# First norm of a two-block fp32 transformer kernel: loaded and turned by quarters, its scale applied behind the products

## The chip, the cores and the metric

The kernel runs on one core of a Trainium2 chip. The time is the device time of one execution in microseconds (us), and the median of several runs counts. In the rows PE is TensorE, PEld its weight load, DVE VectorE, ACT ScalarE, POOL GpSimd and SP SyncE; SPq and POOLq are the queues that issue DMAs. L12 is line 12 of the kernel.

## What is computed

Two transformer blocks on 256 tokens of width 2048, all in fp32. The change touches the start of the first block:

```
u = rmsnorm(h, norm_mix_g[l])            # x * rsqrt(mean(x*x) + eps) * g, per token
z = u @ w_in[l]
b_a, c_a, v_a, q, k, v, gl_a, gl_b = jnp.split(z, SPLIT_POINTS, axis=-1)
y_a = (b_a * centred_dwconv3(c_a * v_a, conv_a_w[l])) @ w_out_a[l]
q = rope(q, s); k = rope(k, s)
att = banded_window_attention(q, k, v, sink_logits[l])
g_a = sigmoid(gl_a + b_gate[:D]);  g_b = sigmoid(gl_b + b_gate[D:])
h = h + (g_a * y_a + g_b * (att @ w_o_attn)) @ w_mix_out
```

Behind it stand the norm, a feed-forward part with a convolution, and a second block with an expert layer. They are not touched.

## The kernel before, in words

**Products by units.** All weights pass through one stream of 1096 units. A unit is 128x1024 fp32 values (512 KB). SP loads it to RAW (5 buffers, L288); ScalarE rounds it to HI (L293); VectorE writes the rest, raw minus HI, to LO (L294). HI and LO have 4 buffers each. TensorE multiplies a unit by the activations, themselves held as a high and a low half (XH and XL in XX), in three passes: L368 to L370 where tokens lie on the partitions of the result (q, k, v), L378 to L380 where channels do. `product` runs over the units of one group of 512 columns, 8 units for 2048 rows, into one of two pairs of banks. A unit by token is 12 matmuls of 512 columns.

**What sets the order.** Each engine has one queue that runs strictly in order, and the program is written out once. Before the matmuls of unit i stand in the queue, `prepare(i + LOOK)` puts HI and LO of the units up to i+3 into the queues of ScalarE and VectorE (LOOK = 3). After each unit `step` adds one piece of the generators in `evacuations`, `beside` and `background`. A product is followed by what takes its banks away.

**The start.** SP loads x in two halves by tokens (L225), the identity (L226) and the norm's factors for all partitions (L227), then the first five units. POOL waits for the factors and loads constants, parameters and small tensors (L228, L229, L233). ScalarE sums the squares of both halves (`squares`, L467), `scale_of` and `rstd` make y, the reciprocal root, on two numbers per partition (L497, L452 to L458). `normed` then works by quarters of the width: VectorE forms x times y times the factors in UN (`scaled`, L503), TensorE turns four 128x128 blocks for each half of the tokens (L527), ScalarE copies the high half to XX (L533), VectorE the low half (L534). All four quarters come before the first unit.

**The first products.** Two products make q, one makes k and v. Behind each, `rope` rotates with four VectorE operations for each half of the tokens (L778, L779, L781, L783), by the tables cos and sin in CONST. For k and v a copy of k (L798) and ScalarE's copy of v (L799) follow. Then come, for each of two halves of the convolution, c (ScalarE copies it to CT, L822), v_a (multiplied with CT to PR, L825), three taps (L830, L813, L815), and b_a (L834); then four products with the gates of the first branch (`gate`: ScalarE's sigmoid from the banks, L842), the product with w_out_a, and for the second branch gate and attention output by turns. The attention runs between the units as `background`. `turned` and `spread` are there for the later norms: `turned` multiplies a quarter by the factors without y and turns it, `spread` makes y a row for all partitions by a diagonal (L568) and two matmuls (L574) into RS (L579).

Of the kernel before, what the change touches and what calls it, by code (L numbers as in the profile page):

```python
# [12 lines left out]
ALU = mybir.AluOpType  # L13
# [96 lines left out]
def _program(nc, a, out, ctx):  # L110
# [101 lines left out]
    def landing(name):  # L212
        return [sem(name), 0]

    l_x = landing("l_x")
    l_xt = [landing(f"l_x{t}") for t in range(2)]
    l_ident, l_const, l_par, l_small, l_gb, l_gb1, l_bi, l_gb2, l_keys, l_out = [landing("l_" + n) for n in (
# [10 lines left out]
    m_const = PO.dma(lambda e: e.dma_start(CONST[:, 128:N_CONST], a["consts"][:, 128:N_CONST]), l_const, m_gb)  # L228
    m_par = PO.dma(lambda e: e.dma_start(PAR[:], a["params"]), l_par, m_gb)  # L229
    for dst, src in ((SINK[:, 0, :], rows(a["sinks"][0])), (SINK[:, 1, :], rows(a["sinks"][1])),  # L230
                     (QKG[:, 0, :], rows(a["qkg"][0])), (QKG[:, 1, :], rows(a["qkg"][1])),
                     (POSI[:], a["pos"])):
        m_small = PO.dma(lambda e, dst=dst, src=src: e.dma_start(dst, src), l_small)  # L233


    units = []
# [41 lines left out]
    landed, hi_done, lo_done, mm_done = [], [], [], []  # L278

    def prepare(n):  # L280

        while len(hi_done) <= min(n, len(units) - 1):
            i = len(hi_done)
            while len(landed) <= min(i + NRAW - 1, len(units) - 1):
                j = len(landed)
                free = [hi_done[j - NRAW], lo_done[j - NRAW]] if j >= NRAW else None
                src, w = units[j]
                landed.append(SP.dma(lambda e, j=j, src=src, w=w: e.dma_start(RAW[:, j % NRAW, 0:w], src),  # L288
                                     l_raw[j % NRAW], free))
# [56 lines left out]
    def product(by_token, nk, xh, xl, ready, k0=0, width=512, turn=0):  # L346
# [44 lines left out]
    def product_both(ready, dst, rest, free):  # L391
# [149 lines left out]
    def turned(g, gb, m_in, m_g, free, marks, m_un, m_un_read):  # L541
# [7 lines left out]
        for t in range(2):  # L549
            i, b, fr = spare()  # L550

            def fn(e, t=t, b=b):
                for j in range(4):
                    m = e.transpose(b[:, 128 * j:128 * j + 128], UN[:, t, 512 * g + 128 * j:512 * g + 128 * j + 128],
                                    ident)
                return m

            m = PE.do(fn, m_u[t], fr)
# [209 lines left out]
    turn = un[:, 3072:3584]  # L768
    cosv, sinv = (const(n).rearrange("p (t c) -> p t c", t=2) for n in ("cos", "sin"))
    m_rope = []  # L770

    def rope(dst, src, t, nh, m):
# [13 lines left out]
    for g in range(2):  # L786
        pair, banks, m = product(True, 16, XH, XL, x_ready)
        free = []
        for t in range(2):
            r, _ = rope(q_tok[:, t, 512 * g:512 * g + 512].rearrange("p (h d) -> p h d", d=64),  # L790
                        banks[t].rearrange("p (h d) -> p h d", d=64), t, 8, m)
            free.append(r)
        acc_free[pair] = free
    pair, banks, m = product(True, 16, XH, XL, x_ready)
    free = []
    for t in range(2):
        r, w = rope(k_tok[:, t, :, 0:64], banks[t][:, 0:256].rearrange("p (h d) -> p h d", d=64), t, 4, m)
# [902 lines left out]
```

How the kernel before makes its waits and increments, by code:

```python
    def wait(self, *marks):  # L74
        for m in marks:
            if m is None:
                continue
            if isinstance(m, list):
                self.wait(*m)
                continue
            sem, value = m
            if self.passed.get(id(sem), 0) < value:
                self.passed[id(sem)] = value
                self.queue.append(lambda e, sem=sem, value=value: e.wait_ge(sem, value))
# [1 line left out]
    def do(self, fn, *marks):  # L86
        self.wait(*marks)
        self.n += 1
        self.queue.append(lambda e: fn(e).then_inc(self.sem, 1))
        return (self.sem, self.n)
# [1 line left out]
    def dma(self, fn, landing, *marks):  # L92
        self.wait(*marks)
        landing[1] += 16
        self.queue.append(lambda e: fn(e).then_inc(landing[0], 16))
        return (landing[0], landing[1])
```

## Time and profile before

| | us |
|---|---|
| median of 3 runs | 3324.21 |
| lowest and highest run | 3323.56, 3326.57 |
| the profiled execution | 3327.32 |
| span of its instructions | 3325.5 |
| TensorE busy in it (98%) | 3255.3 |
| VectorE, ScalarE busy | 2281.4, 1550.7 |

The span runs from the first to the last instruction. The busy time of TensorE is modelled at the ends of matmuls, so it says that TensorE always has work, not that it runs at its peak. A wait is put down to the instruction that came last. PEclk in a row of the stretches is the granted clock of TensorE as a share of 2.4 GHz, so 0.50 is its lower level of 1.2 GHz; a stretch before the first record of the clock shows 1.00 whatever it was.

### The profile page before, as it was taken

How to read it: one execution, taken by the hardware profiler on the slowest of the kernel's cores; microseconds unless marked ns; L12 is line 12 of the kernel's file. 1: busy time of each engine (PE TensorE's matmuls, PEld its weight loads, DVE VectorE, ACT ScalarE, POOL GpSimd, SP SyncE). 2: the span in 40 equal slices, each digit the busy share in tenths (PEclk: the TensorE clock that was granted, in tenths of full speed). 3: DMA queues.
4: the chain of work that ended last, by engine and by line, in shares of the span. 5: the costliest groups of instructions: out<-in, count | busy, mean ns of one | idle time of the engine just before them, and what ended most of it. 6: DMA issues, size and time to landing. Idle time of an engine off the chain costs nothing.

```text
span 3325.5 us, 52769 instructions
## 1 busy us (share of the span) xinstructions
PE 3255.3 (98%) x20926; PEld 2875.0 (86%) x20926; DVE 2281.4 (69%) x3250; ACT 1550.7 (47%) x1988; POOL 5.6 (0%) x14
## 2 busy tenths in 40 slices
PE   7999999999999999998999999999999999999999
PEld 6999999888888888887789999888888888888887
DVE  5664445677577567788659997578787577865554
ACT  4554344555355455554544544444343444434453
POOL 0000000000000000000000000000000000000000
PEclk9999999999999999998999999999999999999999
DMA  6545565655556655552445554554555655555555
GB/s 230 159 146 193 187 209 185 203 190 194 192 179 195 195 187 176 181 168 77 143 155 165 171 172 141 184 171 150 188 177 184 188 185 178 182 186 190 190 190 165
DMA packets 161253, 590.51 MB, mean 178 GB/s; under 512 B 17904, under 2 KB 18064, under 8 KB 159728
## 3 DMA queue, kind: packets, MB, share of 16 engines
q1 hardware_dynamic: 160192, 583.14, 54.5%
q8 instruction: 168, 2.75, 0.3%
q0 software_dynamic: 816, 3.98, 0.3%
q14 instruction: 77, 0.63, 0.1%
HBM read 584.96 MB, written 2.10 MB: 177 GB/s over the span
## 4 chain that ended last, share of the span: by engine, by line
PE 90%; DVE 7%; ACT 2%; issue 1%; DMA 0%; DVEq 0%; SPq 0%; ACTq 0%
PE PS L410 19%; PE PS L368 12%; PE PS L370 12%; PE PS L369 12%; PE PS L413 10%; PE PS L378 7%; PE PS L379 7%; PE PS L380 7%; DVE LO L294 2%; PE PS L1456 1%; DVE GB L1071 1%; PE PS L1467 1%; PE PS L717 0%; ACT UN L672 0%; ACT HI L293 0%
## 5 line engine op out<-in xcount | busy, mean ns | idle before, releaser
L294 DVE TENSOR_TENSOR LO<-RAW,HI 128x1024 fp32r<-128x1024 f32 x1096 | 1327.6, 1218 | 770.3 <-ACT HI L293 768.0
L293 ACT ACTIVATE HI<-RAW 128x1024 fp32r<-128x1024 f32 x1096 | 1150.5, 1055 | 1176.0 <-PE PS L370 606.8
L410 PE MATMUL PS<-XX,HI 128*128 128x512 f32 x2688 | 735.5, 395 | 0.0
L368 PE MATMUL PS<-HI,FH 128*128 128x512 f32 x1632 | 644.1, 395 | 5.8 <-DVE FL L584 5.4
L370 PE MATMUL PS<-HI,FL 128*128 128x512 f32 x1632 | 636.9, 390 | 0.0
L378 PE MATMUL PS<-XX,HI 128*128 128x256 f32 x2176 | 624.1, 287 | 12.2 <-DVE LO L294 9.4
L369 PE MATMUL PS<-LO,FH 128*128 128x512 f32 x1632 | 635.7, 390 | 0.0
L379 PE MATMUL PS<-XX,HI 128*128 128x256 f32 x2176 | 616.3, 283 | 0.0
L380 PE MATMUL PS<-XX,LO 128*128 128x256 f32 x2176 | 616.1, 283 | 0.0
L410 PEld LDWEIGHTS PS<-XX,HI 128*128 128x128 f32 x2688 | 459.6, 189 | 61.9
L413 PEld LDWEIGHTS PS<-XX,LO 128*128 128x128 f32 x2688 | 412.4, 189 | 57.2
L378 PEld LDWEIGHTS PS<-XX,HI 128*128 128x128 f32 x2176 | 418.1, 192 | 20.0 <-issue 14.2
L413 PE MATMUL PS<-XX,LO 128*128 128x256 f32 x2688 | 427.5, 281 | 0.0
L379 PEld LDWEIGHTS PS<-XX,HI 128*128 128x128 f32 x2176 | 418.4, 192 | 0.1
L380 PEld LDWEIGHTS PS<-XX,LO 128*128 128x128 f32 x2176 | 418.1, 192 | 0.0
L368 PEld LDWEIGHTS PS<-HI,FH 128*128 128x128 f32 x1632 | 306.8, 188 | 69.2 <-ACT FH L583 5.9
L370 PEld LDWEIGHTS PS<-HI,FL 128*128 128x128 f32 x1632 | 306.7, 188 | 65.7
L369 PEld LDWEIGHTS PS<-LO,FH 128*128 128x128 f32 x1632 | 306.9, 188 | 61.7
L1440 DVE TENSOR_TENSOR OH<-KEYS,TAB 128x1024 bf16<-128x1024 bf16 x128 | 87.8, 686 | 22.2 <-PE PS L1456 21.9
L897 DVE TENSOR_TENSOR RES<-PS,RES 128x512 f32<-128x512 f32 x112 | 72.0, 685 | 20.7 <-PE PS L370 20.5
L1071 DVE SCALAR_TENSOR_TENSOR GB<-HP,PAR,GB 128x256 f32<-128x256 f32 x180 | 75.7, 479 | 0.0
L368 PE MATMUL PS<-HI,XX 128*128 128x512 f32 (+1 forms) x192 | 72.0, 375 | 3.0 <-DVE LO L294 3.0
(274 smaller groups left out, 2267.8 us busy)
## 6 DMA issues: line engine op xcount, KB each, us to landing
RAW<-in_peer_v SPq DMA_DIRECT2D x256, 512.0 KB, 4.0
RAW<-in_ffn_w_up SPq DMA_DIRECT2D x176, 512.0 KB, 4.3
RAW<-in_peer_ut_rest SPq DMA_DIRECT2D x160, 512.0 KB, 3.9
RAW<-in_w_in SPq DMA_DIRECT2D x136, 512.0 KB, 3.7
RAW<-in_peer_ut SPq DMA_DIRECT2D x96, 512.0 KB, 3.5
RAW<-in_ffn_w_down SPq DMA_DIRECT2D x88, 512.0 KB, 4.3
RAW<-in_w_mix_out SPq DMA_DIRECT2D x32, 512.0 KB, 4.3
RAW<-in_w_in_2c SPq DMA_DIRECT2D x32, 512.0 KB, 4.1
```

The source lines that it names most:

```text
L293: hi_done.append(AC.do(lambda e, raw=raw, hi=hi: e.activation(hi, raw, ACT.Copy), landed[i], used))
L294: lo_done.append(DV.do(lambda e, raw=raw, hi=hi, lo=lo: e.tensor_tensor(lo, raw, hi.bitcast(F32), ALU.subtract), hi_done[i], landed[i], used))
L368: e.matmul(o, x, hi[:, k, :], start=f, stop=False, skip_group_check=True)
L369: e.matmul(o, x, lo[:, k, :], start=False, stop=False, skip_group_check=True)
L370: m = e.matmul(o, y, hi[:, k, :], start=False, stop=l, skip_group_check=True)
L378: e.matmul(o, h, x, start=f, stop=False, skip_group_check=True)
L379: e.matmul(o, h, y, start=False, stop=False, skip_group_check=True)
L380: m = e.matmul(o, w, x, start=False, stop=l, skip_group_check=True)
L410: e.matmul(o, hi[:, k, w], XX[:, 4 * u + k, :, :].rearrange("p h s -> p (h s)"), start=u == 0 and k == 0, stop=False, skip_group_check=True)
L413: m = e.matmul(o[:, 0:S], lo[:, k, w], XH[:, 4 * u + k, :], start=False, stop=u == 3 and k == 3, skip_group_check=True)
L1071: m_cv[c] = DV.do(lambda e, c=c, k=k: e.scalar_tensor_tensor(out=CV[:, c, :], in0=HP[:, c, k:k + S], scalar=par("cw2", 31 * c + k), in1=CV ...
L1440: m_oh = DV.do(lambda e: e.tensor_tensor(OH2[:, k], KEYS2[:].unsqueeze(1).to_broadcast([128, 4, 128, 2]), pairs(1, 128), ALU.is_equal), m_ ...
```

## The change

- SP's first transfers are the identity and then x and the factors by quarters of the width, with the first five units between them. POOL's loads wait for all four quarters of x.
- The first norm goes through `turned`: x times the factors, without y. Quarter 0 is turned before the first unit; quarters 1 to 3 are put in `beside`, in two pieces each (multiply; turn and split), so they come behind units 0 to 5. The matmuls of a unit wait for the quarter that they read.
- `first_scale` is the last in `beside`: behind unit 6 the squares and y; behind unit 7 cos and sin times y (CSY), the row RS of y and its square RR.
- The look-ahead is 1 unit during the first product, and 3 again once the rotation of its result is written.
- What comes out of the products with XX takes y: q and k by CSY, v by ScalarE's scale, c by RR (now on VectorE, for c and v_a together), the convolution by RS, the gates by RS on VectorE ahead of the sigmoid.

The core of the diff:

```diff
-    m_x = [SP.dma(lambda e, t=t: e.dma_start(RES[:, t, :], xin[:, t, :]), l_xt[t]) for t in range(2)]
     m_ident = SP.dma(lambda e: e.dma_start(CONST[:, 0:128], a["consts"][:, 0:128]), l_ident)
-    m_gb = SP.dma(lambda e: e.dma_start(GB[:], rows(a["norms"][0])), l_gb)
...
+    def load_quarter(q):
+        c = slice(512 * q, 512 * q + 512)
+        m_gq.append(SP.dma(lambda e: e.dma_start(GB[:, c], rows(a["norms"][0, c])), l_gq[q]))
+        m_xq.append(SP.dma(lambda e: e.dma_start(RES[:, :, c], xin[:, :, c]), l_xq[q]))
+
+    load_quarter(0)
...
+    land(0)
+    load_quarter(1)
+    land(2)
+    load_quarter(2)
+    land(4)
+    load_quarter(3)
+    m_const = PO.dma(lambda e: e.dma_start(CONST[:, 128:N_CONST], a["consts"][:, 128:N_CONST]), l_const, m_xq)
+    m_par = PO.dma(lambda e: e.dma_start(PAR[:], a["params"]), l_par)
...
+    look = [1]
...
-            prepare(i + LOOK)
+            prepare(i + look[0])
...
-    for t in range(2):
-        squares(RES[:, t, :], t, 0, UN[:, t, :], m_x[t])
-    x_ready, m_un, m_un_read = normed(scale_of(1, m_ssq[0]), GB, m_gb, None, m_ident)
+    x_ready = lambda k: first_marks[k // 4]
...
+    def first_scale():
+        for t in range(2):
+            m_sq0.append(squares(RES[:, t, :], t, 0, STAGE[:, 8 * t:8 * t + 8, :].rearrange("p c s -> p (c s)"), m_xq))
+        y, m_y = scale_of(1, m_sq0)
+        yield
...
+            m_cs.extend(DV.do(lambda e, i=i, t=t, raw=raw: e.tensor_scalar(CSY[:, i, t, :], raw[:, t, :], y[:, t:t + 1],
+                                                                           None, ALU.mult), m_y, m_const)
+                        for t in range(2))
+        m_r.append(spread(y, m_y, RD[:], RS[:], m_const))
+        m_rr.append(DV.do(lambda e: e.tensor_tensor(RR[:], RS[:], RS[:], ALU.mult), m_r))
+        yield
+
+    quarters = [turned(q, GB, m_xq[q], m_gq[q], None, x_marks, m_un, m_un_read) for q in range(4)]
+    for _ in quarters[0]:
+        pass
+    beside.extend(quarters[1:])
+    beside.append(first_scale())
...
         acc_free[pair] = free
+        look[0] = LOOK
...
-        acc_free[pair] = m_ct = [AC.do(lambda e, i=i, b=banks[i]: e.activation(CT[:, 2 * i:2 * i + 2, :], two(b),
-                                                                              ACT.Copy), m, m_y) for i in range(2)]
+        acc_free[pair] = m_ct = [DV.do(lambda e, i=i, b=banks[i]: e.tensor_tensor(
+            CT[:, 2 * i:2 * i + 2, :], two(b), RR[:].unsqueeze(1).to_broadcast([128, 2, S]), ALU.mult), m, m_y, m_rr)
+            for i in range(2)]
...
+        m_cv = DV.do(lambda e: e.tensor_tensor(CT, CT, RS[:].unsqueeze(1).to_broadcast([128, 4, S]), ALU.mult), m_cv,
+                     m_r)
...
+        m_v = [DV.do(lambda e, i=i: e.tensor_tensor(dst[:, 2 * i:2 * i + 2, :], two(banks[i]),
+                                                    RS[:].unsqueeze(1).to_broadcast([128, 2, S]), ALU.mult), m, *more)
+               for i in range(2)]
```

**SP, first transfers.** Before: x, identity, factors, then the units (L225 to L288).

```order
L225 DMA RES<-in_x 128x2048 x2
L226 DMA CONST<-in_consts 128x128
L227 DMA GB<-in_norms 128x2048
L288 DMA RAW<-in_w_in 128x1024 x79
```

The same queue now:

```order
L228 DMA CONST<-in_consts 128x128
L233 DMA GB<-in_norms 128x512
L234 DMA RES<-in_x 128x2x512
L288 DMA RAW<-in_w_in 128x1024
L233 DMA GB<-in_norms 128x512
L234 DMA RES<-in_x 128x2x512
L288 DMA RAW<-in_w_in 128x1024 x2
```

A quarter of factors and a quarter of x stand ahead of the first unit, where all of both stood.

**ScalarE, from the first norm to the first product.** Before, with squares, root, the eight copies of the norm and then units only:

```order
L467 ACTIVATE UN,SM<-RES 128x2048 x2
L454 ACTIVATE SM<-SM 128x2
L533 ACTIVATE XX<-PS 128x4x128 x8
L293 ACTIVATE HI<-RAW 128x1024 x27
```

Now (L604 is the copy of `turned`, L314 HI of a unit, L488 the squares, L475 the root, L589 the diagonal for `spread`, L600 its result):

```order
L604 ACTIVATE XX<-PS 128x4x128 x2
L314 ACTIVATE HI<-RAW 128x1024
L488 ACTIVATE STAGE,SM<-RES 128x2048 x2
L475 ACTIVATE SM<-SM 128x2
L314 ACTIVATE HI<-RAW 128x1024
L589 ACTIVATE RD<-CONST,SM 128x128 x2
L600 ACTIVATE RS<-PS 128x256
L314 ACTIVATE HI<-RAW 128x1024 x18
```

The copies shown are those of quarter 3, the units are 7, 8 and from 9 on: the squares and the root moved to between HI of unit 7 and HI of unit 8.

**VectorE, end of the first product.** Before, LO of eleven units stood ahead of the first rotation:

```order
L294 TENSOR_TENSOR LO<-RAW,HI 128x1024 x11
L778 TENSOR_TENSOR UN<-PS,CONST 128x512
L779 TENSOR_TENSOR UN<-PS,CONST 128x8x32
L781 TENSOR_TENSOR UN<-PS,CONST 128x8x32
L783 TENSOR_TENSOR UN<-UN 128x512
```

Now (L315 is LO, L794 and L798 make CSY and RR, L820 to L825 rotate; a line of dots stands for the rotation's other half):

```order
L315 TENSOR_TENSOR LO<-RAW,HI 128x1024
L794 TENSOR_SCALAR CSY<-CONST,SM 128x64 x4
L798 TENSOR_TENSOR RR<-RS 128x256
L820 TENSOR_TENSOR UN<-PS,CSY 128x512
L821 TENSOR_TENSOR UN<-PS,CSY 128x8x32
L823 TENSOR_TENSOR UN<-PS,CSY 128x8x32
L825 TENSOR_TENSOR UN<-UN 128x512
...
L315 TENSOR_TENSOR LO<-RAW,HI 128x1024 x10
```

The first row is LO of unit 8, the last begins with LO of unit 9: units 9 and 10 moved from ahead of the rotation to behind it.

## Rows read from the trace of the kernel before

**Rows 1.** The page: busy time by engine, and the chain that ended last.

```profile
PE 3255.3 (98%) x20926; PEld 2875.0 (86%) x20926; DVE 2281.4 (69%) x3250; ACT 1550.7 (47%) x1988; POOL 5.6 (0%) x14
...
PE 90%; DVE 7%; ACT 2%; issue 1%; DMA 0%; DVEq 0%; SPq 0%; ACTq 0%
```

**Rows 2.** Waits of TensorE from 90 to 1300 us: total, times, longest.

```profile
PE PS L602 <- DVE UN L798: 0.6, 1, 0.6
```

**Rows 3.** Timeline of the start: start us, us, engine, line, count [idle before, releaser].

```profile
0.74 0.86 SPq L225 DMA_DIRECT2D RES<-in_x  x2
...
8.27 1.91 ACT L467 ACTIVATE UN<-RES 128x2048 f32<-128x2048 f32 x1 [0.49 <-DMA RES<-in_x]
...
10.91 0.20 ACT L454 ACTIVATE SM<-SM 128x2 f32<-128x2 f32 x1 [0.64 <-DVE SM L453]
...
12.54 3.68 PE L527 MATMUL PS<-CONST,UN 128*128 128x128 f32 x16 [12.54 <-DVE UN L503]
...
13.70 0.60 ACT L533 ACTIVATE XX<-PS 128x512 fp32r<-128x512 f32 x1 [2.58 <-PE PS L527]
14.40 1.48 DVE L534 TENSOR_TENSOR XX<-PS,XX 128x512 fp32r<-128x512 f32 x2
...
16.59 1.32 PE L527 MATMUL PS<-CONST,UN 128*128 128x128 f32 x8 [0.37 <-DVE UN L503]
...
20.96 3.88 ACT L293 ACTIVATE HI<-RAW 128x1024 fp32r<-128x1024 f32 x4
22.04 4.63 DVE L294 TENSOR_TENSOR LO<-RAW,HI 128x1024 fp32r<-128x1024 f32 x4
...
23.41 0.63 PE L368 MATMUL PS<-HI,XX 128*128 128x512 f32 x1 [2.98 <-DVE LO L294]
```

**Rows 4.** Stretches: busy us of each engine (count), PEclk, DMA share, GB/s.

```profile
5.00:10.00 5.00, 0.00 (x0) 0.00 (x0) 0.00 (x0) 3.73 (x3) 0.00 (x0) 1.00 1.01 419
23.56:26.98 3.42, 3.42 (x9) 2.68 (x10) 3.11 (x3) 1.28 (x2) 0.00 (x0) 0.50 0.74 217
90.00:230.00 140.00, 139.45 (x1145) 133.09 (x1145) 88.37 (x120) 80.44 (x158) 0.00 (x0) 1.00 0.49 153
1307.00:1310.30 3.30, 3.30 (x9) 2.53 (x8) 1.16 (x2) 0.00 (x0) 0.00 (x0) 0.50 0.71 182
1501.60:1508.30 6.70, 3.25 (x16) 3.28 (x17) 5.43 (x14) 2.09 (x3) 0.00 (x0) 0.50 0.60 194
1578.60:1588.00 9.40, 5.38 (x32) 4.46 (x32) 6.13 (x20) 9.40 (x33) 0.00 (x0) 1.00 0.00 0
2085.00:2092.00 7.00, 3.77 (x30) 3.54 (x30) 5.45 (x5) 4.58 (x6) 0.00 (x0) 1.00 0.22 75
```

**Rows 5.** Line L544, VectorE: ns of one (min/median/max), first and last start.

```profile
L544 DVE TENSOR_TENSOR UN<-RES,GB x16: 683/684/693, 560.1 to 1372.5; 128x512 f32<-128x512 f32 x16
```

**Rows 6.** Timeline of VectorE around the end of the first product.

```profile
47.09 0.69 DVE L778 TENSOR_TENSOR UN<-PS,CONST 128x512 f32<-128x512 f32 x1 [0.34 <-PE PS L370]
...
51.28 3.64 DVE L294 TENSOR_TENSOR LO<-RAW,HI 128x1024 fp32r<-128x1024 f32 x3
56.41 1.23 DVE L294 TENSOR_TENSOR LO<-RAW,HI 128x1024 fp32r<-128x1024 f32 x1 [1.49 <-ACT HI L293]
59.13 1.23 DVE L294 TENSOR_TENSOR LO<-RAW,HI 128x1024 fp32r<-128x1024 f32 x1 [1.49 <-ACT HI L293]
```

**Rows 7.** Line L568, ScalarE, in the same form.

```profile
L568 ACT ACTIVATE RD<-CONST,SM x2: 386/386/387, 631.3 to 631.6; 128x128 f32<-128x128 f32 x2
```

**Rows 8.** Waits of TensorE from 1300 us on: total, times, longest.

```profile
PE PS L378 <- DVE LO L294: 9.4, 12, 1.7
...
PE PS L368 <- DVE FL L584: 5.4, 4, 1.9
PE PS L602 <- DVE KD L1185: 5.4, 1, 5.4
...
PE PS L693 <- ACT UN L682: 4.2, 3, 3.0
```

More of the change, by code:

```diff
@@ L163, in _program @@
     RS = over("RS", [128, S], 38 * K)
+    CSY = over("CSY", [128, 2, 2, 64], 34 * K)
+    RR = over("RR", [128, S], 36 * K)
     RD = over("RD", [128, 2, 128], 39 * K)
@@ L215, in _program @@
     l_x = landing("l_x")
-    l_xt = [landing(f"l_x{t}") for t in range(2)]
+    l_xq = [landing(f"l_x{q}") for q in range(4)]
+    l_gq = [landing(f"l_g{q}") for q in range(4)]
     l_ident, l_const, l_par, l_small, l_gb, l_gb1, l_bi, l_gb2, l_keys, l_out = [landing("l_" + n) for n in (
@@ L224, in _program @@
     xin = a["x"].rearrange("(t p) d -> p t d", p=128)
-    m_x = [SP.dma(lambda e, t=t: e.dma_start(RES[:, t, :], xin[:, t, :]), l_xt[t]) for t in range(2)]
     m_ident = SP.dma(lambda e: e.dma_start(CONST[:, 0:128], a["consts"][:, 0:128]), l_ident)
-    m_gb = SP.dma(lambda e: e.dma_start(GB[:], rows(a["norms"][0])), l_gb)
[L228 to L233, printed above, removed]
+    m_gq, m_xq = [], []
+    def load_quarter(q):
[3 more added lines that the diff above has]
+    load_quarter(0)
     units = []
@@ L278, in _program, with land @@
     landed, hi_done, lo_done, mm_done = [], [], [], []
+    def land(n):
+        while len(landed) <= min(n, len(units) - 1):
+            j = len(landed)
+            free = [hi_done[j - NRAW], lo_done[j - NRAW]] if j >= NRAW else None
+            src, w = units[j]
+            landed.append(SP.dma(lambda e, j=j, src=src, w=w: e.dma_start(RAW[:, j % NRAW, 0:w], src),
+                                 l_raw[j % NRAW], free))
+    land(0)
[6 more added lines that the diff above has]
+    m_par = PO.dma(lambda e: e.dma_start(PAR[:], a["params"]), l_par)
+    for dst, src in ((SINK[:, 0, :], rows(a["sinks"][0])), (SINK[:, 1, :], rows(a["sinks"][1])),
+                     (QKG[:, 0, :], rows(a["qkg"][0])), (QKG[:, 1, :], rows(a["qkg"][1])),
+                     (POSI[:], a["pos"])):
+        m_small = PO.dma(lambda e, dst=dst, src=src: e.dma_start(dst, src), l_small)
+    look = [1]
     def prepare(n):
@@ L283, in prepare @@
             i = len(hi_done)
[L284 to L289, printed above, removed]
+            land(i + NRAW - 1)
             w = units[i][1]
@@ L400, in product_both @@
             i = len(mm_done)
-            prepare(i + LOOK)
+            prepare(i + look[0])
             hi = HI[:, i % NHI, :].rearrange("p (k n) -> p k n", k=4)
@@ L556, in fn @@
                 return m
-            m = PE.do(fn, m_u[t], fr)
+            m = PE.do(fn, m_u[t], fr, m_ident)
             m_un_read.append(m)
@@ L759, in _program @@
     root_table()
-    for t in range(2):
-        squares(RES[:, t, :], t, 0, UN[:, t, :], m_x[t])
-    x_ready, m_un, m_un_read = normed(scale_of(1, m_ssq[0]), GB, m_gb, None, m_ident)
+    x_marks, m_un, m_un_read = [None] * 4, [], []
+    first_marks = x_marks
+    x_ready = lambda k: first_marks[k // 4]
+    m_sq0, m_r, m_rr, m_cs = [], [], [], []
+    cosv, sinv = (CSY[:, i] for i in range(2))
+    def first_scale():
[3 more added lines that the diff above has]
+        yield
+        for i, name in enumerate(("cos", "sin")):
+            raw = const(name).rearrange("p (t c) -> p t c", t=2)
+            m_cs.extend(DV.do(lambda e, i=i, t=t, raw=raw: e.tensor_scalar(CSY[:, i, t, :], raw[:, t, :], y[:, t:t + 1],
[9 more added lines that the diff above has]
+    beside.append(first_scale())
     m_gb_read = m_un
@@ L768, in _program @@
     turn = un[:, 3072:3584]
-    cosv, sinv = (const(n).rearrange("p (t c) -> p t c", t=2) for n in ("cos", "sin"))
     m_rope = []
@@ L798, in _program @@
         m_rope.append(DV.do(lambda e, t=t: e.tensor_copy(k_tok[:, t, :, 64:128], k_tok[:, t, :, 0:64]), w))
-        free += [r, AC.do(lambda e, t=t, b=banks[t]: e.activation(V1[:, t, :], b[:, 256:512], ACT.Copy), m, r)]
+        free += [r, AC.do(lambda e, t=t, b=banks[t]: e.activation(V1[:, t, :], b[:, 256:512], ACT.Copy,
+                                                                        scale=SM[:, 12 + t:13 + t]), m, r)]
     acc_free[pair] = free
-    box1 = {"sc_free": m_un}
+    box1 = {"sc_free": [m_un, m_sq0]}
     sc1 = RES[:].rearrange("p t (h k) -> p (t h) k", k=256)
@@ L841, in gate @@
     def gate(dst, g, banks, m, off, *more):
-        return [AC.do(lambda e, c=c: e.activation(dst[:, c, :], two(banks[c // 2])[:, c % 2, :], ACT.Sigmoid,
-                                                  bias=par("bg", off + 4 * g + c)), m, m_par, *more)
-                for c in range(4)]
+        m_v = [DV.do(lambda e, i=i: e.tensor_tensor(dst[:, 2 * i:2 * i + 2, :], two(banks[i]),
+                                                    RS[:].unsqueeze(1).to_broadcast([128, 2, S]), ALU.mult), m, *more)
+               for i in range(2)]
+        return m_v, [AC.do(lambda e, c=c: e.activation(dst[:, c, :], dst[:, c, :], ACT.Sigmoid,
+                                                       bias=par("bg", off + 4 * g + c)), m_v[c // 2], m_par)
+                     for c in range(4)]
     m_ga = []
@@ L848, in _program @@
         pair, banks, m = product(False, 16, XH, XL, x_ready)
-        acc_free[pair] = gate(GA[:, 4 * g:4 * g + 4, :], g, banks, m, 0)
-        m_ga.append(acc_free[pair])
+        acc_free[pair], m_g = gate(GA[:, 4 * g:4 * g + 4, :], g, banks, m, 0)
+        m_ga.append(m_g)
     m_ya = []
@@ L868, in _program @@
         pair, banks, m = product(False, 16, XH, XL, x_ready)
-        m_g = gate(GT[:], g, banks, m, 16, m_gt)
-        acc_free[pair] = m_g
+        acc_free[pair], m_g = gate(GT[:], g, banks, m, 16, m_gt)
         if g == 3:
```

2 lines of the change are left out of this document (1 added, 1 removed).

## The prediction

> **What bounds the kernel now.** I read the page first. TensorE is busy for 98% of the span and is 90% of the chain that ended last [rows 1]. So time comes only from what TensorE does, or from stretches in which it waits. The waits of TensorE by stretch come second: between 90 and 1300 us there is one of 0.6 us [rows 2]. The start is different. Its first transposition is at 12.54 us and its first matmul of a unit at 23.41 [rows 3]; nothing of the products lies beside that time, so each microsecond there counts in full.
>
> Third, the pace of a unit. VectorE's LO of one unit follows the next at 56.41 and 59.13 us [rows 6], so a unit by token takes 2.72 us, 0.227 for each of its 12 matmuls. At the start the clock is at the lower of its levels for 3.42 us [rows 4], which costs half of that, 1.7. Unit 8, the first of the second product, thus starts at 23.41 + 8 x 2.72 + 1.7 = 46.9, which fits the rotation's start at 47.09 [rows 6], and unit 9 at 49.6. From there on TensorE never waits, so the change is worth what it moves unit 9 by, if what lies behind stays covered.
>
> **The change part by part. Data.** Up to the first quarter SP asks for 0.07 MB of identity, 0.26 of factors and 0.52 of x. The second half of x (2.10 MB with the first) landed at 8.27 [rows 3] at 419 GB/s [rows 4], so data flow from about 3.3 us, and 0.85 MB land at 5.3. The first unit lands 1.25 us later, at 6.5. The rows are 2 KB where x and factors had 8 KB. No row shows such transfers alone: the bounds are the measured rate (0) and half of it, if a 2 KB row took as long as the 4 KB row of a unit (0.79 MB, +1.9 us). I take 0, as the stream beside it has shown one rate for rows of 4 and 8 KB. Later quarters are needed 9 us and more after they land. POOL's loads now wait until about 17 us; the constants are first needed behind 43.
>
> The Trainium skill, page "DMA: Bandwidth & Descriptors", section Specifications, gives about 358 GB/s as what HBM grants a core, and 435 for the fabric. Row and rule differ, 419 against 358, and the measurement decides. By 358 the first quarter would land 0.4 us later and my sum would be 0.4 us higher.
>
> **First quarter to first matmul.** Multiplying by the factors is L544's form, 0.68 us [rows 5], so TensorE turns from 6.1. The transpositions start at 12.54 and the second half's split ends at 14.40 + 1.48 = 15.88 [rows 3]: 3.34 us, at the low clock (16 took 3.68, later 8 took 1.32). ScalarE is free for HI of unit 0 after its second copy, at 8.65. From HI to first matmul it was 23.41 - 20.96 = 2.45 [rows 3]. Unit 0 starts at 11.1 instead of 23.4: **-12.3**. I take the same 3.4 us of low clock behind it; a second stretch as long would add 1.7 us.
>
> **Quarters 1 to 3** were turned ahead of the first matmul and now lie between units 1 and 2, 3 and 4, 5 and 6. The multiplications are covered by the unit ahead. The rest is not: the next unit reads what is turned. At the full clock that is 0.66 us for four transpositions, 0.60 + 0.60 for ScalarE's two copies, 0.68 for the last split, and 0.24 of hand-overs [rows 3]: 2.78 each, of which TensorE idles 1.7. **+8.3** for three. Unit 8 could now start at 46.9 - 12.3 + 8.3 = 42.9.
>
> **The squares** stand on ScalarE between HI of units 7 and 8, and the look-ahead is 1 there. Unit 6 starts at 37.4, and quarter 3's copies end 0.9 before, at 36.5. HI of unit 7 takes 1.05, so the squares start at 37.5; each takes 1.91 and the reading of its sum, some 2.0. From the second's start to the end of the root it is 10.91 + 0.20 - 8.27 = 2.84 [rows 3], so HI of unit 8 starts at 42.35 and unit 8 at 44.8, not 42.9: **+1.9**. The diagonal (2 x 0.39 us [rows 7]) and the two matmuls of `spread` fit in that stop.
>
> **The rotation** was covered: LO of units 8 to 10 had been made ahead of it. Now only that of unit 8 is. VectorE is through with it at 44.7, then come CSY and, behind the matmuls of `spread`, RR, until about 45.5; the rotation takes 51.28 - 47.09 = 4.19 [rows 6], until 49.7. Then LO of unit 9 (1.23 + 0.1), so unit 9 starts at 51.1, while unit 8 was over at 47.5: **+3.6**. Sum: -12.3 + 8.3 + 1.9 + 3.6 = **+1.5**.
>
> **The clock.** That last stop is 3.4 us long. Low clock followed a stop of 3.0 at the start, of 1.9 before 1307 and of 5.4 before 1505; it did not follow one of 3.0 near 1580 and stops of up to 1.7 near 2088 [rows 3, 4, 8]. So it probably falls once around units 8 and 9, for 3.4 us, **+1.7** (bounds 0 and 3.4, if at both stops). Total **+3.2 us**.
>
> **Behind it.** VectorE gets 4 multiplications for c, 16 for the gates (0.68 each) and two of 1024 columns (1.23, LO's form): 16 us over some 400; ScalarE loses 4 copies. From 90 to 230 VectorE is busy for 88 of 140 us [rows 4], and HI and LO are three units (8.2 us) ahead there, while the longest piece added at once is 1.4. Banks go free sooner than the next product of the pair, 11 us on at least. Cost 0; the bounds are 0 and all 16 us. The scaled copy of v costs what the plain one did. The gain cannot hide elsewhere, as this stretch has no wait to fill.
>
> **The rivals.**
> A: the clock stays up at the end of the first product. +1.5 us.
> B, the other way: ScalarE and VectorE are through with units 8 and 9 in time, and only the quarters count: -4.0, or down to -9.0 if these cost only their transpositions (3 x 1.1). For it: both engines idle in much of the first product. Against it: their queues are strict, and the rotation stands ahead of LO of unit 9.
> C, slower: the clock falls at every stop. Place: the three stops of 1.7 us between quarters and the two behind. Each costs up to 1.7: +1.5 + 5 x 1.7 = +10.0. Against it: stops of up to 1.7 near 2088 left the clock up. For it: one of 1.9 ahead of 1307 brought it down, so it decides as soon as the stops between quarters are a little longer than I have them [rows 4, 8].
> D: transfers of 2 KB rows go at half the rate: +3.2 + 1.9 = +5.1.
> E: VectorE's added work reaches TensorE. Place: the convolution, where LO waits behind rotations of taps and attention; from the point at which LO comes over 8.2 us late each microsecond counts, up to 16: +19.
> That the first unit waits for more than the first quarter is no rival of weight: its wait is for the marks of that quarter alone.
>
> **How the numbers follow.** The profiled execution took 3327.3 us, 3.1 above the median of 3324.2. On its own time my forecast is 3330.5; against the median it is 3327.4, which I predict. Chances: the forecast 0.43 (3327.4), A 0.20 (3325.7), B 0.09 (3315.2 to 3320.2), C 0.10 (3334.2), D 0.13 (3329.3), E 0.05 (up to 3343). The range takes in forecast, A, D and the upper part of B, with 1 to 2 us for the length of the low clock on either side: 3318.5 to 3333. A measurement of this kernel can tell about 0.2%, 6.6 us, from no change. Slower than that are C and E, 0.15; faster is the far end of B, 0.04; the rest, 0.81, is the same.
>
> **What would show it.** In the profile of the changed kernel: the first matmul of a unit at about 11 us; three waits of TensorE for the split of a quarter, of some 1.7 us; a wait of about 2 us ahead of unit 8 for its LO, behind the squares; one of 3.4 ahead of unit 9, with the rotation on VectorE in it; the clock at 0.50 once behind these; no new wait from there to 1300 us. Wrong would be a first matmul much behind 11 us (D), a low clock between the quarters (C), or waits for LO in the convolution (E). If unit 9 starts before 47 us, my reading of the order is wrong (B).

## The result, and the profile after

| | before | after |
|---|---|---|
| median, us | 3324.85 | 3331.87 |
| lowest and highest of 19 runs | 3323.56, 3326.9 | 3327.72, 3333.1 |
| span of the profiled execution | 3325.5 | 3330.4 |
| TensorE busy in it | 3255.3 | 3256.7 |

The ratio is 1.0019, with a 95% interval of 1.0013 to 1.0026. By the medians the changed kernel is slower by 7.0 us (by the means, which give the ratio, by 6.3), where 3.2 were forecast. That is inside the range, and about the 0.2% that the prediction took as the least that can be told from no change. The page of after, busy times and chain, answers to [rows 1] with the same shares:

```profile
PE 3256.7 (98%) x20930; PEld 2875.3 (86%) x20930; DVE 2295.5 (69%) x3277; ACT 1548.7 (47%) x1987; POOL 5.6 (0%) x14
...
PE 90%; DVE 7%; ACT 2%; issue 1%; DMA 0%; DVEq 0%; SPq 0%; ACTq 0%
```

So the page does not tell where 7 us went. The waits of TensorE up to 1300 us do (total, times, longest). Before, this stretch had 14.1 us ahead of the transpositions, 3.0 ahead of unit 0, and the 0.6 of [rows 2]. After:

```profile
PE PS L575 <- DVE UN L565: 8.2, 1, 8.2
PE PS L389 <- DVE LO L315: 6.7, 2, 3.7
PE PS L389 <- ACT HI L314: 5.0, 3, 1.7
PE PS L595 <- ACT RD L589: 0.6, 1, 0.6
PE PS L623 <- DVE UN L841: 0.5, 1, 0.5
```

In order of time these are: the wait for the first quarter (8.2), the one for LO of unit 0 (3.0 of the 6.7), three stops of 1.7 between the quarters, 0.6 ahead of `spread`, and 3.7 ahead of unit 9. The last row is the wait of [rows 2]. The timeline of after shows the start and the first stop (start us, us, engine, line, count, [idle before, releaser]):

```profile
7.50 1.29 DVE L565 TENSOR_TENSOR UN<-RES,GB 128x512 f32<-128x512 f32 x2 [6.64 <-DMA RES<-in_x]
...
8.25 1.97 PE L575 MATMUL PS<-CONST,UN 128*128 128x128 f32 x8 [8.25 <-DVE UN L565]
...
10.75 1.05 ACT L314 ACTIVATE HI<-RAW 128x1024 fp32r<-128x1024 f32 x1
...
13.20 0.77 PE L389 MATMUL PS<-HI,XX 128*128 128x512 f32 x1 [2.98 <-DVE LO L315]
...
21.09 1.03 PE L575 MATMUL PS<-CONST,UN 128*128 128x128 f32 x8
21.73 1.09 ACT L604 ACTIVATE XX<-PS 128x512 fp32r<-128x512 f32 x2 [6.96 <-PE PS L575]
...
22.36 1.29 DVE L605 TENSOR_TENSOR XX<-PS,XX 128x512 fp32r<-128x512 f32 x2 [5.30 <-ACT XX L604]
...
23.79 0.47 PE L389 MATMUL PS<-HI,XX 128*128 128x512 f32 x1 [1.66 <-ACT HI L314]
```

The first row gives the landing of quarter 0: the multiplication waits for x until 7.50. The last two give a stop between quarters: TensorE has turned quarter 1, ScalarE and VectorE copy and split it until 23.65, and unit 2 begins at 23.79. The row names HI, but the HI made there is that of a later unit; by these rows the split came last.

The end of the first product on VectorE, against [rows 6]:

```profile
45.93 1.23 DVE L315 TENSOR_TENSOR LO<-RAW,HI 128x1024 fp32r<-128x1024 f32 x1 [0.40 <-ACT HI L314]
47.07 0.74 DVE L794 TENSOR_SCALAR CSY<-CONST,SM 128x64 f32<-128x64 f32 x4
47.76 0.42 DVE L798 TENSOR_TENSOR RR<-RS 128x256 f32<-128x256 f32 x1
48.38 0.69 DVE L820 TENSOR_TENSOR UN<-PS,CSY 128x512 f32<-128x512 f32 x1 [0.19 <-DVE RR L798]
...
51.95 0.69 DVE L825 TENSOR_TENSOR UN<-UN 128x512 f32<-128x512 f32 x1
52.56 4.62 DVE L315 TENSOR_TENSOR LO<-RAW,HI 128x1024 fp32r<-128x1024 f32 x4
```

One LO (unit 8) stands ahead of the rotation, and the next four come behind it, in one block. TensorE, with unit 8 done at 50.24, waits for the first of the four:

```profile
53.92 0.76 PE L389 MATMUL PS<-HI,XX 128*128 128x512 f32 x1 [3.68 <-DVE LO L315]
54.48 0.63 PE L390 MATMUL PS<-LO,XX 128*128 128x512 f32 x1
```

Its matmuls then take 0.63 us and start 0.43 apart, not 0.227. The stretches show why (columns as in [rows 4]: busy us of each engine, PEclk, DMA share, GB/s):

```profile
53.92:59.12 5.20, 5.20 (x12) 4.10 (x13) 3.26 (x3) 0.00 (x0) 0.00 (x0) 0.50 0.74 231
59.20:62.00 2.80, 2.80 (x14) 2.29 (x13) 1.22 (x1) 1.06 (x1) 0.00 (x0) 1.00 0.82 306
90.00:230.00 140.00, 139.46 (x1116) 132.34 (x1115) 91.81 (x124) 79.74 (x155) 0.00 (x0) 1.00 0.48 155
1312.90:1316.30 3.40, 3.40 (x15) 2.81 (x16) 2.12 (x2) 0.79 (x2) 0.00 (x0) 1.00 0.42 112
```

The clock is at its lower level for the whole of unit 9. In 90 to 230 us VectorE is busy for 91.8 us, where it was 88.4, and no wait comes of it: the list above has none there but the old 0.5. From 1300 us on the waits are those of [rows 8], within 0.1 us. The fourth row is a difference of this one execution: at the place that [rows 4] shows at 0.50 around 1307, the clock stayed at 1.00 here. Up to there the shift is unchanged: the matmul behind that wait starts at 1306.04 before and at 1312.89 after. The fall that only the execution of before has gives back some 1.7 us, and the spans end 4.9 apart where the medians are 7.0 apart.

The starts of the units put it together. Units 0 to 10 began before at 23.41, 27.83, 30.57, 33.30, 36.02, 38.73, 41.45, 44.17, 46.90, 49.62 and 52.34; now at 13.20, 18.33, 23.79, 26.63, 32.05, 34.86, 40.29, 43.10, 47.21, 53.92 and 59.16. Unit 0 is 10.2 us earlier, unit 10 is 6.8 later. Later places keep this distance: the attention's first transposition is at 100.86 after and at 94.00 before.

### The profile page after: what moved, and what is told of

The parts are those of the page before. It is cut to its first block, busy times and chain, and to the rows that moved or that the text cites. A ratio compares the mean times of both kernels' runs of the same rounds, so it can differ in the third digit from the quotient of the medians.

```text
span 3330.4 us, 52830 instructions
## 1 busy us (share of the span) xinstructions
PE 3256.7 (98%) x20930; PEld 2875.3 (86%) x20930; DVE 2295.5 (69%) x3277; ACT 1548.7 (47%) x1987; POOL 5.6 (0%) x14
## 4 chain that ended last, share of the span: by engine, by line
PE 90%; DVE 7%; ACT 2%; issue 1%; DMA 0%; DVEq 0%; SPq 0%; ACTq 0%
PE PS L431 19%; PE PS L389 12%; PE PS L391 12%; PE PS L390 12%; PE PS L434 10%; PE PS L399 7%; PE PS L400 7%; PE PS L401 7%; DVE LO L315 2%; PE PS L1505 1%; DVE GB L1120 1%; PE PS L1516 1%; ACT HI L314 1%; PE PS L738 0%; ACT UN L693 0%
## 5 line engine op out<-in xcount | busy, mean ns | idle before, releaser
L315 DVE TENSOR_TENSOR LO<-RAW,HI 128x1024 fp32r<-128x1024 f32 x1096 | 1326.3, 1217 | 746.2 <-ACT HI L314 743.9
L314 ACT ACTIVATE HI<-RAW 128x1024 fp32r<-128x1024 f32 x1096 | 1149.2, 1054 | 1163.3 <-PE PS L391 596.1
```

## Experiments

All are edits of the changed kernel. "The kernel before" ran beside them on the same chip, with medians from 3324.46 to 3324.69.

**The squares moved up.** They come behind units 2 and 4 and the root behind unit 5, where they all stood behind unit 6.

```diff
+    def first_squares(t):
+        m_sq0.append(squares(RES[:, t, :], t, 0, STAGE[:, 8 * t:8 * t + 8, :].rearrange("p c s -> p (c s)"), m_xq))
...
-    beside.extend(quarters[1:])
-    beside.append(first_scale())
+    def pieces():
+        for todo in ([n(1)], [n(1)], [n(2), lambda: first_squares(0)], [n(2)], [n(3), lambda: first_squares(1)], [first_root, n(3)], [], [lambda: next(last)]):
+            for f in todo:
+                f()
+            yield
```

> The changed kernel with one part moved: ScalarE's two squares stand behind units 2 and 4, where ScalarE idles, and the root behind unit 5; the look-ahead stays 1. Theory (the squares cost only the stop ahead of unit 8, the rotation costs the stop ahead of unit 9): the wait ahead of unit 8 goes (about 1.6 us in the changed kernel), but unit 9 still waits for its LO behind the rotation, which starts when the first product ends, so unit 9 moves by about 1 us only, from 53.9 to about 52.9, and the clock still falls there. Time 1 us below the changed kernel, about 3331. Rival (the squares cause both stops): unit 9 moves by 4 to 5 us and the time to about 3326.

Measured: 3330.46 us (3329.58 to 3331.93, 10 runs), ratio to before 1.0017 [1.0008, 1.0027]. The 0.65 ahead of `spread` is gone, and unit 8 begins at 46.21. Unit 9 begins at 53.07 after a longer stop of 3.87:

```profile
53.07 0.77 PE L389 MATMUL PS<-HI,XX 128*128 128x512 f32 x1 [3.87 <-DVE LO L315]
```

So of the 1.0 us gained ahead of unit 8 there is 0.85 left at unit 9, and the stop there is no shorter. The squares are a small part of the loss; the stop ahead of unit 9 does not come from them.

**The look-ahead back at 3 ahead of the rotation.** On top of the edit above: from unit 6 on the units are prepared three ahead, so that LO of units 9 and 10 stands in front of the rotation, as before the change (VectorE writes eleven LO ahead of it).

```diff
+            if i == 6:
+                look[0] = LOOK
```

> As e1, and the look-ahead goes back to 3 units at unit 6 instead of behind the first rotation, so HI and LO of units 9 and 10 are made ahead of the rotation. Theory: both stops at the end of the first product are gone, unit 9 starts at about 49.0 (before: 49.6; changed kernel: 53.9), no low clock between the first and the second unit stretch, so 4.9 us and 2.6 us of clock: about 3324.5. Rival (the quarters between the units make the loss, or VectorE's added work later): stays within 2 us of the changed kernel, above 3329.

Measured: 3324.47 us (3323.01 to 3325.79, 10 runs), ratio 0.9999 [0.9989, 1.0009]. Waits of TensorE up to 1300 us:

```profile
PE PS L577 <- DVE UN L567: 8.4, 1, 8.4
PE PS L391 <- ACT HI L314: 5.0, 3, 1.7
PE PS L391 <- DVE LO L315: 3.0, 1, 3.0
PE PS L625 <- DVE UN L857: 0.5, 1, 0.5
```

The stop of 3.7 is gone, and with it the low clock: unit 9 begins at 49.49 and unit 10 at 52.21. Against the run with the squares alone, that edit is worth 5.0 us in unit 10 (57.23 to 52.21) and 6.0 in the median. (The two profiled executions also differ by one fall of the clock behind it: 0.96 against 1.00 from 1290 to 1330 us.) The place of LO behind the rotation is what made the changed kernel slower than the one before.

**The quarters turned one unit ahead.** Look-ahead 2 during the first product, each quarter multiplied and turned at once behind units 0, 2 and 4, one unit before it is read; squares and root behind unit 6.

```diff
-    look = [1]
+    look = [2]
...
+        for todo in ([n(1), n(1)], [], [n(2), n(2)], [], [n(3), n(3)], [], [lambda: first_squares(0), lambda: first_squares(1), first_root], [lambda: next(last)]):
```

> The changed kernel with quarters 1 to 3 turned one unit earlier (behind units 0, 2, 4 instead of 1, 3, 5) so that a unit of matmuls lies between turning and use, and a look-ahead of 2 instead of 1 in the first product; squares and the rest as in the changed kernel. Theory: the three stops of 1.7 us between quarters go or shrink below 0.5, 8 transpositions of 1.1 us each stay, and LO of one unit more stands ahead of the rotation, so the stop ahead of unit 9 goes too and one of about 1 to 2 us comes ahead of unit 10: about 8 us less, 3322 to 3325. Rival (TensorE waits for the data of x, not for the split): the stops stay, 3329 or more.

Measured: 3321.11 us (3318.57 to 3323.2, 10 runs), ratio 0.9986 [0.9977, 0.9996]. There is no stop between quarters, 0.77 us ahead of `spread` and 0.85 ahead of unit 10, which begins at 48.46, 3.9 us before its place in the kernel before. A quarter that is split while a unit still multiplies costs about its transpositions (1.03 us for eight): with quarter 2 or 3 turned in it, the way from one unit to the next took 3.52 us, against 2.72 without.

**The clock kept up.** Between units 8 and 9 TensorE does 14 matmuls of 512 columns on XX into a spare bank; nobody reads them. They fill the stop and are done before LO of unit 9 is.

```diff
+            if i == 9:
+                j, b, fr = spare()
...
+                    for n in range(BUSY):
+                        m = e.matmul(b, XX[:, n % 4, 0, 0:128], XX[:, 4 + n % 4, :, :].rearrange("p h s -> p (h s)"),
+                                     start=True, stop=True, skip_group_check=True)
```

> The changed kernel with 14 extra matmuls of 512 columns (3.2 us, operands from XX, result unused) put on TensorE between units 8 and 9, where it waits 3.7 us. All waits stay as they are. Theory: the stop itself cannot shrink, but the clock does not fall behind it: unit 9 starts at 53.9 as before, and the 5.2 us at half speed behind it go, so 2.6 us less: about 3329.3. Rival (the low clock is not set off by this stop, or costs nothing): 3332 as the changed kernel, or more.

Measured: 3329.36 us (3328.11 to 3330.8, 10 runs), ratio 1.0014 [1.0004, 1.0023]. Timeline and stretch:

```profile
50.16 3.33 PE L410 MATMUL PS<-XX 128*128 128x512 f32 x14
54.02 0.47 PE L390 MATMUL PS<-HI,XX 128*128 128x512 f32 x1 [0.53 <-DVE LO L316]
```

```profile
54.02:60.00 5.98, 5.98 (x26) 4.96 (x27) 4.49 (x4) 1.22 (x2) 0.00 (x0) 1.00 0.78 245
```

Unit 9 begins at the same time (54.02 against 53.92), yet unit 10 at 56.86 instead of 59.16: 2.84 us later, not 5.24. So the clock alone cost 2.4 us here, apart from the stop; the median fell by 2.5.

**All three edits together.** Look-ahead 2 and then 3 from unit 6, quarters at once, squares behind units 3 and 5.

```diff
-    look = [1]
+    look = [2]
...
+            if i == 6:
+                look[0] = LOOK
...
+        for todo in ([n(1), n(1)], [], [n(2), n(2)], [lambda: first_squares(0)], [n(3), n(3)], [lambda: first_squares(1)], [first_root], [lambda: next(last)]):
```

> Early squares, look-ahead 2 and from unit 6 on 3, and quarters turned a unit ahead, together. By the theory TensorE has no stop of over 0.6 us between its first unit at 13.2 and unit 9; unit 9 starts at 13.2 + 1.7 of low clock + 9 x 2.72 + 3 x 1.1 of transpositions = 42.7, 6.9 us ahead of the kernel before (49.6). Time 3324.7 - 6.9 = 3317.8, ratio 0.998. Rival (a stop moves elsewhere, since HI and LO of the next units now follow the split): only as fast as the variant that turns a unit ahead, 3321.

Measured: 3320.98 us (3319.16 to 3322.52, 11 runs), ratio 0.9986 [0.9977, 0.9996]: 3 us more than expected, and unit 9 begins at 45.01, not 42.7. Two stops were new, each from the same cause at another place. With two units prepared ahead, the multiplication of quarter 3 stood behind LO of unit 6 (0.94 us ahead of the transposition at 31.28). The diagonal for `spread` stood on ScalarE behind HI of unit 10 (1.03 ahead of 41.74).

**Why the first quarter landed late.** Three edits on the first loads, one execution each; their times tell nothing (the profiled executions of all kernels here differ by up to 4.4 us behind unit 10), so they are read at the start only. First the factors' 2 KB of one row for all partitions are replaced by each partition's own 2 KB of x (this leaves the factors out of the first norm):

```diff
-        m_gq.append(SP.dma(lambda e: e.dma_start(GB[:, c], rows(a["norms"][0, c])), l_gq[q]))
+        m_gq.append(SP.dma(lambda e: e.dma_start(GB[:, c], xin[:, 0, c]), l_gq[q]))
```

> The changed kernel with the factors' transfers replaced: each partition reads its own 2 KB row of x instead of all partitions reading one row of factors. Same sizes, same places in SBUF; the norm's factors are wrong, so the result is. Theory A (128 reads of one place are what slows the first 3 us): the multiplication of quarter 0 starts at 5.5 to 6 instead of 7.5. Theory B (transfers of 2 KB rows are slow while the stream starts up, whatever they read): it stays at 7 to 8.

Then x ahead of the factors in each quarter:

```diff
-        m_gq.append(SP.dma(lambda e: e.dma_start(GB[:, c], rows(a["norms"][0, c])), l_gq[q]))
         m_xq.append(SP.dma(lambda e: e.dma_start(RES[:, :, c], xin[:, :, c]), l_xq[q]))
+        m_gq.append(SP.dma(lambda e: e.dma_start(GB[:, c], rows(a["norms"][0, c])), l_gq[q]))
```

> The changed kernel with x ahead of the factors in each quarter. If the factors' transfer is what is slow at the start (A), the stream is up to speed while x moves, and slow behind it; if the start-up is slow for 2 KB rows of either kind (B), nothing changes: the quarter is complete at 7.5, within 0.3, and the first unit starts at 13.2.

And two halves in place of four quarters, in rows of 4 KB:

```diff
+        if q % 2:
+            return
+        c = slice(512 * q, 512 * q + 1024)
+        m_gq.extend([SP.dma(lambda e: e.dma_start(GB[:, c], rows(a["norms"][0, c])), l_gq[q])] * 2)
+        m_xq.extend([SP.dma(lambda e: e.dma_start(RES[:, :, c], xin[:, :, c]), l_xq[q])] * 2)
```

> The changed kernel with x and factors loaded by halves of the width (4 KB rows, two transfers each twice as large); the turning is still by quarters. If 4 KB rows keep the full rate from 3.3 us on, 0.07 + 1.57 MB land at 3.3 + 1.64/0.419 = 7.2 us, and the first multiplication starts no later than with quarters (7.5): size of the rows is what the start lacks. If the first microseconds are slow whatever the rows are (at the 117 to 162 GB/s seen up to 5 us), it starts at 9 or later.

Measured: first multiplications at 6.58, 7.67 and 9.05 us, times 3329.72, 3330.37 and 3329.98. The stretch from 2 to 5 us moved 145 GB/s in the changed kernel and 350 in the kernel before (422 from 3 us on):

```profile
2.00:5.00 3.00, 0.00 (x0) 0.00 (x0) 0.00 (x0) 0.22 (x2) 0.00 (x0) 1.00 0.68 145
```

```profile
2.00:5.00 3.00, 0.00 (x0) 0.00 (x0) 0.00 (x0) 0.22 (x2) 0.00 (x0) 1.00 0.91 350
```

With other rows for the factors, and with halves:

```profile
2.00:5.00 3.00, 0.00 (x0) 0.00 (x0) 0.00 (x0) 0.22 (x2) 0.00 (x0) 1.00 0.69 207
```

```profile
2.00:5.00 3.00, 0.00 (x0) 0.00 (x0) 0.00 (x0) 0.22 (x2) 0.00 (x0) 1.00 0.89 220
5.00:8.00 3.00, 0.00 (x0) 0.00 (x0) 0.00 (x0) 0.00 (x0) 0.00 (x0) 1.00 0.98 359
```

The halves were expected at 7.2 and landed at 9.03: with 4 KB rows the first 3 us are slow as well, so the rows' length alone is not the cause. With x first the quarter was complete no earlier, but its stretches differ:

```profile
3.00:4.00 1.00, 0.00 (x0) 0.00 (x0) 0.00 (x0) 0.00 (x0) 0.00 (x0) 1.00 0.96 338
4.00:5.00 1.00, 0.00 (x0) 0.00 (x0) 0.00 (x0) 0.00 (x0) 0.00 (x0) 1.00 0.42 129
5.00:6.00 1.00, 0.00 (x0) 0.00 (x0) 0.00 (x0) 0.00 (x0) 0.00 (x0) 1.00 0.60 211
```

Here 2 KB rows of x move at 338 GB/s as early as 3 us. The rate falls at 4 us, when by the bytes moved (0.6 MB, as much as identity and x) the factors are next, and the DMA engines are then busy for only 0.42 of the time. That is what the expectation says for its case A, the factors' transfer as the slow one. The run with other rows for the factors agrees in part: its quarter landed at 6.55, where seven kernels with the same first loads as the changed one gave 7.4 to 7.7 six times and 6.87 once, and it moved 207 GB/s from 2 to 5 us against their 137 to 163. But it is still far from 350. So the factors' row, which all partitions read, probably has a part in it; one execution each does not show it, and the rest is open.

**No stop left.** Quarters 2 and 3 are multiplied one unit before they are turned. `first_scale` has one more `yield`, behind CSY, so that `spread` and RR come two units later than CSY, behind unit 9; the rotation of q needs only CSY.

```diff
+        yield
...
-        for todo in ([n(1), n(1)], [], [n(2), n(2)], [lambda: first_squares(0)], [n(3), n(3)], [lambda: first_squares(1)], [first_root], [lambda: next(last)]):
+        for todo in ([n(1), n(1)], [n(2)], [n(2)], [lambda: first_squares(0), n(3)], [n(3)], [lambda: first_squares(1), first_root], [], [lambda: next(last)], [], [lambda: next(last)]):
```

> e5 with its two new stops (0.9 us ahead of quarter 3, whose multiplication stood behind LO of unit 6; 1.0 us ahead of the matmuls of spread) taken away: the multiplications of quarters 2 and 3 one step earlier, the root straight behind the squares, spread two units later. Expected: no stop of TensorE over 0.6 us between 13.3 and the first rotation, unit 9 at 42.7 (e5: 45.0, before: 49.6), so 6.9 us below the kernel before, about 3317.7, and 2 to 3 us below e5. Rival: the stops come back at other instructions, 3320 or more.

Measured: **3317.5 us** (3317.08 to 3320.08, 11 runs), ratio 0.9978 [0.9969, 0.9987]. This beats both kernels: 7.1 us under the kernel before and 14.4 under the changed one. Waits up to 1300 us, and the stretch from unit 0 to unit 10:

```profile
PE PS L577 <- DVE UN L567: 7.6, 1, 7.6
PE PS L391 <- DVE LO L315: 3.0, 1, 3.0
PE PS L391 <- DVE FL L607: 1.9, 1, 1.9
PE PS L625 <- DVE UN L858: 0.5, 1, 0.5
```

```profile
12.59:44.31 31.72, 31.72 (x148) 26.44 (x149) 25.02 (x41) 19.19 (x25) 3.85 (x7) 1.00 0.86 296
```

TensorE is busy for all of the 31.72 us. (PEclk shows 1.00 because the first record of the clock comes later; six matmuls of unit 0 took 0.63 us or more.) In the changed kernel the same ten units took 45.96 us, with 36.65 busy. (The wait for FL is at the block's end, near 1299 us; it is one of [rows 8] that now falls on this side of 1300.) Unit 10 begins at 44.31, 8.0 before its place in the kernel before.

**The loads as before, in that kernel.** x by halves, then identity and factors whole; all else as in the last one.

```diff
-        m_gq.append(SP.dma(lambda e: e.dma_start(GB[:, c], rows(a["norms"][0, c])), l_gq[q]))
-        m_xq.append(SP.dma(lambda e: e.dma_start(RES[:, :, c], xin[:, :, c]), l_xq[q]))
+        if q:
+            return
+        halves = [SP.dma(lambda e, t=t: e.dma_start(RES[:, t, :], xin[:, t, :]), l_xq[t]) for t in range(2)]
+        ids.append(SP.dma(lambda e: e.dma_start(CONST[:, 0:128], a["consts"][:, 0:128]), l_ident))
+        m_gq.extend([SP.dma(lambda e: e.dma_start(GB[:], rows(a["norms"][0])), l_gq[0])] * 4)
+        m_xq.extend([halves] * 4)
```

> e9 with one part undone: x in two halves, identity and all factors are loaded ahead of the units, as in the kernel before. The factors then land at 10.9, so the first multiplication is at 11.0 and the first unit at 11.0 + 5.7 = 16.7 instead of 13.2. Loading by quarters is then worth 3.5 us: e10 = e9 + 3.5, about 3321. Rival (the start of the units is set by the first weights, which now land at 12.2): unit 0 at 17 or later and more than 4 us over e9.

Measured: 3322.52 us (3320.94 to 3323.76, 10 runs), ratio 0.9994 [0.9984, 1.0003]. Unit 0 begins at 16.52 instead of 12.59, unit 10 at 48.67 instead of 44.31. The start of unit 0 is as expected (16.7); the 5.0 us in the median are more than the 3.5 expected. So loading by quarters is worth 4.4 us by the start of unit 10 and 5.0 by the medians, in spite of its slow start, and the rest of the change (the quarters turned without y, between the units) 3.7 by the one and 2.1 by the other. Why the two differ is open.

**The identity behind the first quarter.** The load of the identity moves behind the load of quarter 0.

> e9 with the identity (64 KB in 512 byte rows) loaded behind quarter 0 of x and factors instead of first. If the small rows of the first transfer hold the stream up while it starts, quarter 0 is complete at 6.5 or earlier instead of 7.5 and everything moves by 1 us. If the start-up is slow for any 2 KB rows, quarter 0 gains the 0.2 us of its bytes only and the time is that of e9.

Measured: 3318.61 us (3316.5 to 3319.71, 10 runs), ratio 0.9979 [0.997, 0.9989]. Quarter 0 landed at 6.54 and unit 0 began at 12.26, 0.3 earlier; unit 10 began 0.1 earlier, and the time is the same as without this edit. The landing fits the first case of the expectation, which counted from 7.5, but the kernel without this edit had landed at 6.87; the gain of 0.3 is nearer to the 0.2 of the second case.

## Why the prediction was right in part, step by step

**What bounds the kernel** was right: TensorE, and the change is worth what it moves the units of the first two products by. The shift of unit 10 was 6.8 us, that of the medians 7.0.

**The sum, term by term**, to the start of unit 10:

| | forecast, us | measured, us | off by |
|---|---|---|---|
| unit 0 begins | 11.1 | 13.20 | +2.1 |
| unit 0 to 1, low clock in it | 4.4 | 5.13 | +0.7 |
| unit 1 to 7, three quarters in it | 24.6 | 24.77 | +0.2 |
| unit 7 to 8, squares | 4.7 | 4.11 | -0.6 |
| unit 8 to 9, rotation | 6.3 | 6.71 | +0.4 |
| unit 9 to 10, low clock | 4.4 | 5.24 | +0.8 |
| unit 10 begins | 55.5 | 59.16 | +3.6 |

The forecast +3.2 and these +3.6 give the measured +6.8. The path was right at each step, and two sizes carry the error: the landing of the first quarter (+2.1) and the two stretches of low clock (+1.5). Both were on the slow side, so the forecast caught less than half of the loss; the result is inside the range because the range had room for D and for a longer low clock. Its number alone (3331.9) lies nearer to C (3334.2) and D (3329.3) than to the forecast (3327.4). The traces tell them apart.

**Data: the mis-sized term.** The step was "data flow from about 3.3 us, and 0.85 MB land at 5.3", at the 419 GB/s of [rows 4]. The quarter landed at 7.48: from 2 to 5 us the stream gave 145 GB/s. I had named this case as D and taken half the rate as its bound, +1.9; it came out at +2.2. But the reason given there, the 2 KB rows, did not stand up alone: with 4 KB rows the stream began slowly too. The rate of [rows 4] is that of 5 to 10 us, and it did hold for the head of the kernel before: 422 GB/s from 3 to 5 us, with the first half of x (1.05 MB) landed by 5.78:

```profile
5.78 1.91 ACT L467 ACTIVATE UN<-RES 128x2048 f32<-128x2048 f32 x1 [3.54 <-DMA RES<-in_x]
```

What failed is the step from those loads to these: a stream that began with x in 8 KB rows gave the rate, and I carried it to one that begins with the identity, the factors' row for all partitions and 2 KB rows. From there on the chain was right: from the landing to unit 0 it is 5.7 us, forecast 5.7 (5.4 to 11.1).

By the 358 GB/s of the Trainium skill, page "DMA: Bandwidth & Descriptors", section Specifications, the quarter would have landed at 5.7, an estimate, and still 1.8 us early.

**Quarters 1 to 3: right.** Three stops of 1.66 us, forecast 1.7; from unit 1 to unit 2 it is 5.46 us, forecast 2.72 + 2.78 = 5.50.

**The squares: right, 0.5 too dear.** Unit 8 began 1.4 us late and not 1.9. The sign that I named, a wait of unit 8 for its LO, is not in the list: the matmuls of `spread` stood in between and waited 0.65 us for their diagonal, which ScalarE made behind HI of unit 8. LO of unit 8 was done at 47.16, 0.05 ahead of the unit's first matmul, so the squares held it as forecast. With squares and root moved up the stop vanished, and 0.85 of it stayed gained at unit 9.

**The rotation: right.** The stop is 3.68 us against 3.4; from start to start, as in the sum, it is 4.0 against 3.6. The difference is CSY and RR, which end 1.0 us behind LO of unit 8 (forecast 0.8), and 0.2 from there to the rotation. The run with the look-ahead back at 3 shows the cause, since that edit alone removes the stop. Rival B, that both engines would be in time, is refuted by the same rows.

**The clock: it fell where I said, and for longer.** Forecast was 3.4 us of low clock, +1.7. The granted clock is 1.00 up to 52.0 us and 0.50 from 52.5 to 59.0, some 6.8 us in all, 5.2 of them under work, and it cost 2.4 by the run that kept TensorE busy. The bound of 3.4 held, though I had got it from two falls and there was one. Rival A is refuted. Rival C, a fall at every stop, is too: the three stops of 1.66 left it up, in this trace and in the six others that have them.

**Behind it: right.** 14 us more of VectorE's work (2295.5 against 2281.4) cost TensorE nothing; rival E is refuted by the list of waits to 1300 us.

**The range** held the median, near its upper end. The measured ratio of 1.0019 has the 0.2% of the prediction within its interval, so the loss is clear of zero but small.

## What to carry to other kernels

A rate of the DMA stream holds for the loads that it was measured with. When other loads come to the head of a kernel (smaller rows, one row read by all partitions), their landing needs a run of its own, or a wide bound: here 350 GB/s became 145, and 2 us were lost. In strictly ordered queues a smaller look-ahead is paid for where a long block (here a rotation of 4.2 us) stands between two units: put back the look-ahead there, give each turned quarter one unit of distance from its reader, move what blocks a queue (here squares and `spread`) to where TensorE has work, and a change that cost 7 us gains 7. A stop of TensorE should be priced with its clock, which here cost 0 to 2.4 us on top of a stop of 3.4 to 3.9.

## What the runs showed of the hardware

- The DMA stream was slow up to 5 us in every kernel that began with small pieces: 137 to 220 GB/s from 2 to 5 us, against 350 and 336 in the two where 8 KB rows of x came first, and 315 to 418 from 5 to 8 us in all. Rows' length and the identity do not explain it alone: with x first, its 2 KB rows moved at 338 GB/s from 3 to 4 us. The rate then fell to 129, which points at the factors' row, but without that row the stream gave only 207. The cause is open.
- How long the clock stays low is not fixed. After nearly the same stop ahead of unit 9, the way from unit 9 to unit 10 took 5.24 us after a stop of 3.68, 4.16 after 3.87, 4.41 after 3.70 (twice: with other rows for the factors, and with x first), and 2.84 after 3.42. In that last one, the halves, the clock never fell:

```profile
54.89 0.47 PE L391 MATMUL PS<-HI,XX 128*128 128x512 f32 x1 [3.42 <-DVE LO L317]
```

```profile
54.89:57.70 2.81, 2.81 (x12) 2.33 (x13) 2.81 (x3) 0.00 (x0) 0.00 (x0) 1.00 0.61 192
```

- The same at the start: 8 matmuls of the first unit took 0.63 us or more in the kernel before, 11 in the changed one and 6 in the one without stops (6 to 12 over all thirteen kernels). The Trainium skill, page "TensorE: Matmul & The Clock Gate", Part 1, says that this number varies from run to run of one kernel. These traces, of different kernels, agree in kind. So a term of 1.7 us for one fall of the clock deserves bounds of 0 and some 2.5, an estimate from the 0 to 2.4 us measured behind unit 9.
